# Hybrid decoder layer on one core: projection tiles in halves, larger margins in the written order, second weights asked for earlier

## The chip, the cores and the metric

The kernel runs on one core of a Trainium2 chip. A core has TensorE (PE) for matmuls, VectorE (DVE), ScalarE (ACT) and GpSimd (POOL) for elementwise work, SyncE (SP) for issuing transfers, and 16 DMA engines. Each engine runs its own instruction list in order and waits on semaphores. The metric is device microseconds of one execution. The profile is one execution recorded by the hardware profiler.

## The reference

One layer of a decoder, float32, for a prompt of 512 positions (4 tiles of 128 rows) and for 8 decode requests of one token each, with a past of 4096 positions.

```
h = RMSNorm(x); z = h @ w_in          # 1024 -> 3584 = u_A, v_A, gate_A, q, k, v, gate_B
a = gelu(u_A) * (tril(W_s) @ RMSNorm_group(gelu(v_A)) + b_s)
b = block attention over q, k, v (8 heads x 64, blocks of 256, ALiBi)
y = concat(RMSNorm(a)*silu(gate_A), RMSNorm(b)*silu(gate_B)) @ w_out
out = x + RMSNorm(y)
```

For the prompt the attention is plain causal attention, since there are only two blocks. For a decode request, every head scores the 16 past blocks of 256 positions by q times the mean of K, takes the best three, and attends to these and to the new token. K and V lie in a paged cache and are reached through a page table. So each request needs all its K (8.4 MB) and only the chosen V rows.

## The kernel before, in words

**Prompt.** The seven 512-wide column chunks of `w_in` are worked in the order k, q, v, u, va, ga, gb (steps `pj`, c = 0 to 6), then the two halves of `w_out` (steps `op`). Each is 4 tiles of 128 rows; a tile sums 8 contraction slices into one of two PSUM banks (PA0, PA1). The constant `QUARTERS`, 4, cuts a tile into four pieces of two slices (`pj0` three times, then `pj`, line 980; `op0`, `op`, line 1070). Between pieces TensorE can do other steps. The weights alternate between two buffers, and each chunk comes in four transfers (`WP`) of 512 KB.

**Other TensorE steps.** `kt`, `qk`, `ptr`, `pv` are the prompt's attention (lines 1008, 1026, 1035, 1047); `sg` is the gating matmul (1015); `spj` and `sfd` project the decode tokens and fold the result (934, 994); `spj` needs the chunk's weights.

**Decode requests.** For each request b, GpSimd issues 16 indirect loads, one for each K block (`ld`, line 842), five in flight. VectorE adds the two halves of each block (`ks`, line 704), and TensorE sums four blocks at a time with a window matmul (`gs`, line 1086, four for each request). VectorE forms the gate scores and picks three blocks (`ga`, from line 1469), then `pg` and four `ex` steps multiply the chosen K by q (line 1516), and `sr` reduces (line 1531). The K buffer is then free and `ld` of the next request may start. Softmax follows with `bc` (line 1093), `mt` (1098, VectorE 1550 and 1553) and `mb` (1102), each a small matmul answered by VectorE, and the value matmuls `pv0` and `pv1` (1115). After request 7 come `fin0` to `fin2` and the decode output projection `fop`, `ffd`.

**The order.** `make_plan` writes the order of every engine before the kernel is built. It keeps a clock for each engine and lists of steps (lanes) with assumed durations and dependencies, and always takes the step that could start first; ties go by lane rank. On TensorE the ranks are gate, score, first, attention, side, sample, project. A step of the lanes gate and score is taken only when its data would have been ready for `MARGIN`, 0.3 us; the first three `gs` of a request wait `EARLY_SUMS`, 1.5 us.

```
reach = {"gate": MARGIN, "score": MARGIN, "spread": MARGIN}
...
hold = reach.get(x[1], 0.0) if eng == "PE" else 0.0
if s[0] == "gs" and s[2] < G - 1:
    hold = EARLY_SUMS
start = max(clock[eng], ready + hold)
```

`LANDED` holds assumed arrival times of the first inputs; ("w", 1, 3) is the last piece of the second weights (chunk q), ("w0", x) the pieces of the first. The first are issued by SP right behind the first x tile, in `QUARTERS` transfers, each with its own semaphore. The second are issued by SP in four pieces, each behind the landing of a K block of request 0: blocks 0, 3, 6, 9. Behind these SP has the stores of the k rows and then the spreading of q. Request 0's gate needs the decode tokens' q, made from the second weights by `spj-1` and `sfd-1`, stored and spread over the partitions (`qst`, `qb-0`).

In the order before, TensorE begins so: transposes of x 0 and of the decode rows, two pieces of tile (0,0), transposes of x 1 to 3, `spj-0`, a piece, `sfd-0`, the last piece, a piece of tile (0,1), `gs-0-0`, `kt-0`, two pieces, `gs-0-1`, the last piece, a piece of tile (0,2), `kt-1`, a piece, `gs-0-2`, `spj-1`.

Of the kernel before, what the change touches and what calls it, by code (L numbers as in the profile page):

```python
# [48 lines left out]
def make_plan():  # L49
# [268 lines left out]
    ends, plan = {}, {eng: [] for eng, _ in lanes}  # L318
    for early, at in LANDED:
        ends["Q", early] = at  # L320
# [3 lines left out]
    while True:  # L324
# [35 lines left out]
        if eng == "PE" and bank(s):  # L360
# [10 lines left out]

FLIGHT, WP, EARLY_SUMS, ROOT_HOLD, LANDS = 5, 4, 1.5, 3.0, 1.5
PLAN_START = {"PE": 3.6, "ACT": 2.8, "DVE": 1.0, "POOL": 6.3, "SP": 18.0, "Q": 12.0}
LANDED = [(("x", 0), 4.3), (("x", 1), 10.5), (("x", 2), 12.5), (("x", 3), 14.5), (("xs",), 5.5), (("w", 1, WP - 1), 36.0),
          (("w0", 0), 5.8), (("w0", 1), 7.2), (("w0", 2), 8.6), (("w0", 3), 10.0)]
TILE_US, KEY_US, LAG, MARGIN, SLACK, QUARTERS = 7.4, 1.65, 0.25, 0.3, 0.05, 4
DVE_LANES = "score gate attention groups norm out scale sample tail"
POOL_LANES = "root tiny load fetch"

# [1 line left out]
def hymba_kernel(nc, x_prompt, x_sample, cache_k, cache_v, page_table, g_pre, w_in, sgu_gain, sgu_w,  # L381
# [34 lines left out]
    with ctx:  # L416
# [6 lines left out]
        def sem(name):  # L423
            return ctx.enter_context(nc.semaphore(name))
# [95 lines left out]
        s_k = [sem(f"k_block_loaded{n}") for n in range(NB)]  # L520
# [90 lines left out]
        def load_w(eng, c, x):  # L611

            kcs = slice(x * KC // WP, (x + 1) * KC // WP)
            eng.dma_start(wbuf[:, c % 2, kcs, :], w_src(c)[:, kcs, :]).then_inc(s_w[c % 2], 16)
# [104 lines left out]
        def _(sp):  # L719
# [15 lines left out]
                             (gain[:, :], sgu_gain.rearrange("l g c -> l (g c)").broadcast_to([P, W]))):  # L735
                sp.dma_start(dst, src, allow_slow_non_contiguous=True).then_inc(s_small, 16)
            for x in range(WP):
                sp.wait_ge(s_k[3 * x], 16)
                load_w(sp, 1, x)
            for s in PLAN["SP"]:  # L740
                kind = s[0]
# [889 lines left out]
```

## Time and profile before

| | |
|---|---|
| median of 3 runs | 479.25 us (479.13 to 482.02) |
| the profiled execution | 475.23 us, its span 473.6 us |
| mean granted TensorE clock | 0.936 |
| busy: TensorE, VectorE, GpSimd, ScalarE | 431.6, 283.0, 244.4, 131.8 us |
| weight load (PEld), beside the matmuls | 191.7 us |
| moved by DMA | 110.96 MB, 234 GB/s over the span |

The span runs from the first to the last instruction; the rest of the execution's time lies around it. The two busiest engines are TensorE with 91% and VectorE with 60%. Each group of matmuls in float32 is recorded as two instructions for a contraction slice, so a whole tile is 16 and a quarter 4. Times in the timelines are microseconds from the start of the span.

### The profile page before, as it was taken

The page shows a single profiled execution, that of the slowest core. Times are in us where ns is not written, and L with a number is a line of the kernel's source. Part 1 is how long each engine was busy: PE and PEld are TensorE (multiplying, and loading weights), DVE is VectorE, ACT ScalarE, POOL GpSimd, SP SyncE. Part 2 cuts the span into 40 slices and gives each one's busy share as a digit, 9 for nine tenths or more (in the row PEclk, how much of TensorE's full clock was granted, in tenths as well). Part 3 has the DMA queues.
Part 4 walks back from the last instruction along what each step waited for, and adds up shares of the span by engine and source line. Part 5 has one row for each costly group of instructions (what it writes and reads, how often), then busy time and mean ns, then how long its engine had stood idle before and what let it go on. Part 6 is the DMA issues. An engine that isn't in the chain of part 4 may idle for free.

```text
span 473.6 us, 7936 instructions
## 1 busy us (share of the span) xinstructions
PE 431.6 (91%) x2264; PEld 191.7 (40%) x2264; DVE 283.0 (60%) x749; ACT 131.8 (28%) x295; POOL 244.4 (52%) x344
## 2 busy tenths in 40 slices
PE   6879998999998999898899998997999979969992
PEld 3323443334333544354244544443444434434430
DVE  1534385458445877786476868685746764681334
ACT  3311210101222256224433538524631101000122
POOL 4877115771676167726582576644571666371021
PEclk9997998999998899998699999996599989988997
DMA  8999169994999389759970899349994699451121
GB/s 259 357 391 339 48 201 339 348 265 137 320 360 331 87 284 342 227 165 319 334 226 13 260 360 354 71 99 381 347 316 128 208 381 376 77 103 33 47 90 47
DMA packets 77083, 110.96 MB, mean 234 GB/s; under 512 B 44952, under 2 KB 45464, under 8 KB 77040
## 3 DMA queue, kind: packets, MB, share of 16 engines
q0 software_dynamic: 22576, 71.45, 43.8%
q1 hardware_dynamic: 42768, 21.14, 17.5%
q10 hardware_dynamic: 11696, 17.87, 11.6%
q8 instruction: 18, 0.29, 0.3%
q14 instruction: 25, 0.20, 0.1%
HBM read 106.11 MB, written 4.29 MB: 233 GB/s over the span
## 4 chain that ended last, share of the span: by engine, by line
PE 30%; DMA 29%; DVE 15%; POOL 10%; issue 9%; DVEq 3%; ACT 1%; POOLq 1%; SPq 1%; ACTq 0%
DMA K<-in_cache_k,kidx 23%; PE PA L980 11%; PE PA L1070 8%; POOL K L842 8%; DVE ksum L1516 5%; PE GB L1086 4%; DMA wbuf<-in_w_in 3%; PE SB L934 2%; DVEq L1514 2%; DMA V<-in_page_table 2%; POOL rstd L856 1%; DMA V<-in_cache_v 1%; DVEq L1515 1%; DVE ksum L1469 1%; PE SB L1026 1%
## 5 line engine op out<-in xcount | busy, mean ns | idle before, releaser
L842 POOL DMA_INDIRECT K<-in_cache_k,kidx x128 | 136.4, 1065 | 143.6 <-DVE ksum L1516 73.5
L980 PE MATMUL PA<-wbuf,hT 128*128 128x512 f32 x384 | 184.9, 623 | 0.0
L704 DVE TENSOR_TENSOR ksum<-K 128x512 f32<-128x512 f32 x128 | 87.5, 690 | 85.7 <-DMA K<-in_cache_k,kidx 69.3
L980 PEld LDWEIGHTS PA<-wbuf,hT 128*128 128x128 f32 x384 | 71.3, 197 | 93.0 <-issue 91.0
L689 POOL DMA_DIRECT2D V<-in_cache_v x128 | 75.8, 592 | 30.6 <-issue 17.1
L1070 PE MATMUL PA<-wbuf,hT 128*128 128x512 f32 x128 | 61.7, 629 | 2.4 <-DVE v L1449 2.4
L1516 DVE TENSOR_TENSOR ksum<-K,qb 128x128 f32<-128x128 f32 x192 | 41.7, 285 | 13.4 <-issue 7.1
L1086 PE MATMUL GB<-ksum,win 128*32 128x512 f32 x256 | 37.6, 662 | 8.0 <-DVE ksum L704 7.8
L1070 PEld LDWEIGHTS PA<-wbuf,hT 128*128 128x128 f32 x128 | 24.3, 200 | 32.9 <-issue 32.4
L980 PE MATMUL PA<-hT,wbuf 128*128 128x512 f32 x64 | 31.1, 630 | 0.0
L1026 PE MATMUL SB<-kT,qT 64*128 64x128 f32 (+3 forms) x64 | 28.7, 534 | 0.8 <-DVE pr L1422 0.8
L1531 DVE TENSOR_REDUCE sc<-ksum 128x48 f32<-128x3072 f32 x8 | 26.8, 3353 | 0.3
L1259 ACT ACTIVATE pr<-pr,smax 128x128 f32<-128x128 f32 (+3 forms) x32 | 17.9, 560 | 30.6 <-DVE smax L1425 30.1
L855 POOL TENSOR_SCALAR rstd<-msum 128x1 f32<-128x1 f32 (+3 forms) x18 | 5.6, 310 | 39.5 <-DVE msum L1452 32.4
L1047 PEld LDWEIGHTS PO<-v,pT 128*128 128x128 f32 x160 | 22.6, 209 | 5.5 <-issue 5.4
L1047 PE MATMUL PO<-v,pT 128*128 128x64 f32 x160 | 23.6, 283 | 0.0
L934 PE MATMUL SB<-wbuf,hTs 128*32 128x512 f32 x144 | 19.0, 649 | 2.4 <-DMA wbuf<-in_w_in 2.4
L1267 ACT COPY pT<-SB 128x128 f32<-128x128 f32 (+3 forms) x32 | 13.4, 422 | 27.4 <-PE SB L1035 27.1
L1259 ACT ACT_TABLE_LOAD x13 | 16.7, 1283 | 7.5 <-PE PA L980 7.2
L980 PEld LDWEIGHTS PA<-hT,wbuf 128*128 128x128 f32 x64 | 11.8, 195 | 15.3 <-issue 15.3
L1035 PE MATMUL SB<-ident,pr 128*128 128x128 f32 x80 | 16.6, 309 | 1.3 <-ACT pr L1259 0.9
L1086 PEld LDWEIGHTS GB<-ksum,win 128*32 128x32 f32 x256 | 5.2, 112 | 30.7 <-DVE ksum L704 18.3
(186 smaller groups left out, 376.8 us busy)
## 6 DMA issues: line engine op xcount, KB each, us to landing
wbuf<-in_w_in ACTq DMA_DIRECT2D x20, 512.0 KB, 6.5
V<-in_cache_v SPq DMA_DIRECT2D x240, 32.0 KB
wbuf<-in_w_in SPq DMA_DIRECT2D x8, 512.0 KB, 8.5
V<-in_cache_v POOLq DMA_DIRECT2D x128, 32.0 KB, 2.6
wbuf<-in_w_out ACTq DMA_DIRECT2D x8, 512.0 KB, 8.8
K<-in_cache_k,kidx POOLq DMA_INDIRECT x128, 8.6
qb<-q_rows SPq DMA_DIRECT2D x8, 256.0 KB, 7.2
ya<-in_x_prompt SPq DMA_DIRECT2D x2, 512.0 KB, 7.0
```

Of the source, the lines that this page charges most:

```text
L689: eng.dma_start(V[j * ROWS:(j + 1) * ROWS, h * TOP + k, :, :], v_pages[bass.ds(page, 1), :, :, h * HD:(h + 1) * HD] .rearrange("a p r d -> ...
L704: eng.tensor_tensor(ksum[:, n % SUMS, :], K[:, n, 0, :], K[:, n, 1, :], ALU.add).then_inc(s_dsum, 1)
L842: pool.indirect_dma_start(K[:, n, :, :].rearrange("p r w -> p (r w)"), None, k_rows, bass.IndirectOffsetOnAxis(ap=kidx[:, b, n:n + 1], axis=0)
L934: last = pe.matmul(bank[32 * j:32 * j + 32, :], src[:, kc, :], w[:, kc, :], start=(kc < 4), stop=(kc >= 4), tile_position=(0, 32 * j))
L980: last = pe.matmul(bank[:, :], lhs, rhs, start=(kc == 0), stop=(kc == KC - 1))
L1026: sb_filled(pe.matmul(bank[:, 0:(i + 1) * P], qT[o:o + HD, h // 2, i * P:(i + 1) * P], kT[o:o + HD, h // 2, 0:(i + 1) * P], start=True, st ...
L1047: last = pe.matmul(PO[:, i * HD:(i + 1) * HD], pT[:, a % 2, jt, :], v[:, jt, h * HD:(h + 1) * HD], start=(jt == 0), stop=(jt == i))
L1070: last = pe.matmul(bank[:, :], hT[:, kc, t * P:(t + 1) * P], wbuf[:, c % 2, kc, :], start=(kc == 0), stop=(kc == KC - 1))
L1086: last = pe.matmul(GB[32 * j:32 * j + 32, :], win[:, 31 - g:63 - g], ksum[:, (4 * g + j) % SUMS, :], start=(g == 0), stop=(g == G - 1), ti ...
L1259: act.activation(pr[:, a % 2, 0:(i + 1) * P], pr[:, a % 2, 0:(i + 1) * P], ACT.Exp, bias=smax[:, a % 2:a % 2 + 1], accum_out=ssum[:, h, i: ...
L1516: last = dve.tensor_tensor(kq[:, h * TOP + k, :, :], K[:, bass.ds(n, 1), :, h * HD:(h + 1) * HD] .rearrange("p a r d -> p (a r) d"), qb[:, ...
L1531: dve.tensor_reduce(sc[:, :, :, :].rearrange("p h k r -> p (h k) r"), kq[:, :, :, :], AX.X, ALU.add).then_inc(s_scr, 1)
```

## The change

Three constants and one wait. `QUARTERS` goes from 4 to 2, so a projection tile is two pieces of four slices, and the first weights come in two transfers of 1 MB. `MARGIN` goes from 0.3 to 1.2. `LANDED` has two arrival times for the first weights and 31.0 in place of 36.0 for the last piece of the second. The four pieces of the second weights wait for blocks 0, 2, 4 and 6. The whole order of every engine is written anew from these values.

```diff
-LANDED = [(("x", 0), 4.3), (("x", 1), 10.5), (("x", 2), 12.5), (("x", 3), 14.5), (("xs",), 5.5), (("w", 1, WP - 1), 36.0),
-          (("w0", 0), 5.8), (("w0", 1), 7.2), (("w0", 2), 8.6), (("w0", 3), 10.0)]
-TILE_US, KEY_US, LAG, MARGIN, SLACK, QUARTERS = 7.4, 1.65, 0.25, 0.3, 0.05, 4
+LANDED = [(("x", 0), 4.3), (("x", 1), 10.5), (("x", 2), 12.5), (("x", 3), 14.5), (("xs",), 5.5), (("w", 1, WP - 1), 31.0),
+          (("w0", 0), 6.5), (("w0", 1), 10.0)]
+TILE_US, KEY_US, LAG, MARGIN, SLACK, QUARTERS = 7.4, 1.65, 0.25, 1.2, 0.05, 2
...
             for x in range(WP):
-                sp.wait_ge(s_k[3 * x], 16)
+                sp.wait_ge(s_k[2 * x], 16)
                 load_w(sp, 1, x)
```

## Rows read from the trace of the kernel before

**Rows 1.** Who waited for whom: engine, line, releaser; us in total, times, longest.

```profile
PE GB L1086 <- DVE ksum L704: 7.8, 5, 3.4
PE DC L1102 <- DVE dgm L1553: 7.4, 4, 2.6
PE SB L952 <- DMA ya<-in_x_prompt: 6.1, 2, 4.6
...
PE SB L1035 <- ACT pr L1259: 0.9, 2, 0.5
...
POOL K L842 <- DVE ksum L1516: 73.5, 7, 19.9
```

**Rows 2.** TensorE by stretch: length, busy (instructions), granted clock, DMA share, GB/s.

```profile
0.00:474.00 474.00, 431.63 (x2264) 0.94 0.73 234
...
79.00:83.00 4.00, 4.00 (x16) 0.63 1.05 381
151.00:157.00 6.00, 6.00 (x16) 0.50 0.78 210
223.00:232.00 9.00, 6.15 (x21) 0.50 1.08 338
324.00:341.00 17.00, 16.50 (x46) 0.51 1.06 360
...
424.00:430.00 6.00, 5.21 (x6) 0.50 0.58 113
...
200.00:204.00 4.00, 4.00 (x62) 1.00 0.22 33
```

**Rows 3.** Timeline of TensorE, four stalls: start, duration, instruction, idle before.

```profile
34.92 1.93 PE L1086 MATMUL GB<-ksum,win 128*32 128x512 f32 x8 [3.45 <-DVE ksum L704]
...
150.91 1.94 PE L1086 MATMUL GB<-ksum,win 128*32 128x512 f32 x8 [1.64 <-DVE ksum L704]
198.19 1.07 PE L1086 MATMUL GB<-ksum,win 128*32 128x512 f32 x8 [1.30 <-DVE ksum L704]
...
323.98 0.35 PE L1102 MATMUL DC<-dgm,one 8*128 8x8 f32 x2 [2.59 <-DVE dgm L1553]
```

**Rows 4.** Timeline of VectorE before the stall at 323.98.

```profile
322.34 0.69 DVE L704 TENSOR_TENSOR ksum<-K 128x512 f32<-128x512 f32 x1 [2.91 <-DMA K<-in_cache_k,kidx]
```

**Rows 5.** Timeline, last sums and gate of request 7.

```profile
404.99 0.68 DVE L704 TENSOR_TENSOR ksum<-K 128x512 f32<-128x512 f32 x1
...
408.33 1.06 PE L1086 MATMUL GB<-ksum,win 128*32 128x512 f32 x8
...
409.46 0.69 DVE L1469 TENSOR_TENSOR ksum<-GB,qb 128x512 f32<-128x512 f32 x1 [3.79 <-PE GB L1086]
```

**Rows 6.** First weights' issues (0 to 1.6, 1.6 to 2.2 us; us to landing), then the timeline.

```profile
wbuf<-in_w_in SPq DMA_DIRECT2D x1, 512.0 KB, 5.7
...
wbuf<-in_w_in SPq DMA_DIRECT2D x2, 512.0 KB, 6.9
...
7.46 5.10 PE L980 MATMUL PA<-wbuf,hT 128*128 128x512 f32 x8
...
13.97 1.09 PE L952 MATMUL SB<-ident,ya 128*128 128x128 f32 x8 [1.41 <-DMA ya<-in_x_prompt]
```

**Rows 7.** Timeline around the second weights: SP's issues, a block sum, the decode matmul.

```profile
20.03 17.15 SPq L614 DMA_DIRECT2D wbuf<-in_w_in  x4
...
32.56 0.69 DVE L704 TENSOR_TENSOR ksum<-K 128x512 f32<-128x512 f32 x1 [1.35 <-DMA K<-in_cache_k,kidx]
...
45.12 0.13 PEld L934 LDWEIGHTS SB<-wbuf,hTs 128*32 128x32 f32 x4 [0.30 <-DMA wbuf<-in_w_in]
```

**Rows 8.** Timeline of the tail: the last reduce, the last transposes of decode rows.

```profile
420.69 3.35 DVE L1531 TENSOR_REDUCE sc<-ksum 128x48 f32<-128x3072 f32 x1
...
453.15 0.41 PE L1129 MATMUL SB<-ident,yas 8*128 8x8 f32 x4 [0.21 <-DVE obs L1584]
```

## The prediction

> **What bounds the kernel now.** I read the table of who waited for whom first, because TensorE is busy for 91% of the span and only its waits can be taken away. Its largest waits are those for block sums (VectorE line 704), 7.8 us in 5 stalls, for the softmax maximum (line 1553), 7.4 us in 4 stalls, and for the first rows of x at the head, 6.1 us [rows 1]. The POOL row of the same group shows the second bound. The next request's K blocks may only be issued when the selected K has been multiplied with q, and GpSimd stood 73.5 us over 7 such waits. So there are two long lines of work. One is TensorE's own load. The other is the request loop: 16 K blocks, their sums, the last window matmul `gs` of the request, the gate `ga` on VectorE, the products `ex`, then the next 16 blocks.
>
> The windows come second, because a stall costs more than its length here. Over the span the granted clock is 0.94. In the stretches at 151, 223, 324 and 424 us it is 0.50 to 0.51 (the 1.2 GHz level) for 6, 9, 17 and 6 us [rows 2], and each comes after TensorE had stood. The stretch at 324 us alone is 16.50 us of busy time at half speed, so 8 us of extra time.
>
> Third, the timeline around single stalls. The last sums of requests 2 and 3 were met 1.64 and 1.30 us too early [rows 3]. The maximum step of request 5 was met 2.59 us too early, and the rows of VectorE say why: its queue has a block sum in front of the maximum, which waited 2.91 us for the next request's K block [rows 3, 4]. All four stalls on line 1553 read like this. In the five requests 1, 4, 5, 6 and 7 it is the other way round. In request 7 the last block sum ends at 405.67, the matmul starts at 408.33, and the gate had waited 3.79 us [rows 5]. Read likewise, the five are late by 0.8, 1.4, 0.4, 2.1 and 2.7 us, together 7.3 us. TensorE is thus early for softmax steps and late for most gate steps.
>
> **The change part by part.** No matmul, evacuation or byte is added or removed. What changes is the order on TensorE (with it on the other engines), the split of the first weight transfer, and when the second weights are asked for.
>
> **A. Head, first weights in two transfers.** The first quarter is issued at 1.37 and lands 5.7 us later, at 7.1. The second row is a median over that one and the next, so the second took about 8.1 us and landed near 10.0 [rows 6]. With halves the first projection waits for both, so it starts near 10.0 in place of 7.46, 2.5 us late. The cover: TensorE next needs x rows that came at 13.97, and it stood 1.41 us for them [rows 6]. The eight half-tile matmuls took 5.10 us, so they end near 15.1, 1.1 us after the x rows. What is left of that is covered by the 3.45 us stall before the matmul at 34.92 [rows 3]. Price 0 here; without that cover, 1.1 us.
>
> The Trainium skill, "Perfetto Trace Analysis", section DMA Optimizations, says that splitting transfers into smaller pieces may let some start sooner, which speaks against this part. By that rule alone the head would lose the 2.5 us; the trace agrees that the quarter came earlier, and shows the two covers above.
>
> **B. Second weights with blocks 0, 2, 4, 6.** SP issued the four pieces between 20.03 and 37.18, the last when block 9 had come, at about 36.8 [rows 7]. Block 6 was summed at 32.56, but with one more 512 KB piece ahead of it it comes some 1.3 us later (my estimate: K blocks came 1.3 to 2 us apart around there, and the queues share the same engines), so the last piece is issued near 33.9. The decode matmul `spj-1` waited for it until 45.12, 8.3 us after its issue [rows 7]. The same latency gives 42.1. Working the planner's rule over the first two tiles, I find `spj-1` directly behind `gs-0-1` and tile (0,1), where before half a tile and `gs-0-2` stood between. TensorE gets there near 37.5 to 38, so it would stand about 4 us for weights. In exchange the stall at `gs-0-1` shrinks from 3.45 to about 1: tile (0,1) is complete before it (1.8 us of cover), A adds about 1, and the block itself is up to 1.3 us later. Sum of A and B: +1.5 us; ends -3 (the order keeps it covered and q is spread sooner) and +5. Krow stores behind the four waits on SP move forward by about 3 us and nobody waits for them there.
>
> **C. Softmax steps 0.9 us further out, thrice in a row.** `bc`, `mt` and `mb` each get 1.2 in place of 0.3, so `mb` is planned up to 2.7 us later against the same VectorE work. The four stalls were 1.7, 0.7, 2.6 and 2.4. I take 5.5 of the 7.4 us [rows 1] away (ends 0 and 7.4). Nothing is queued behind them except the value matmuls of the same request, whose results are only needed at the end.
>
> **D. Last sums of a request.** The two early stalls (2.94 us) shrink to about 1: -2 (ends 0 and -2.9). `EARLY_SUMS`, the hold for the first three sums, is unchanged.
>
> **E. The same matmuls where TensorE is late.** Each may now come 0.9 us later by the margin and on average 0.9 us later by the coarser grid (half of 3.7 less half of 1.85). Over 7 loops that is at most 12.6 us in the request loop, and nothing if all fall well. This delay reaches the end only where TensorE has nothing else. After the last reduce ends at 424.04, 49.5 us follow [rows 8], mostly projections. The dependent chain alone I put at some 35 us: about 7 for the softmax and value steps, 13 for the output rows and their norm up to the transposes at 453.15 [rows 8], and 15 of the 20 us behind these, since in them three quarters of a projection stand between the decode steps. So the loop has about 15 us of room, and I charge +3 (ends 0 and 12.6).
>
> **F. Coarser grid for all small steps.** Attention, decode and evacuation steps can enter only at 3.7 us intervals. VectorE and ScalarE stand longer, at places a two-bank ring runs dry, and the last decode steps interleave with halves. +4.5 us: 1.5 at the tail (one more quarter between `fin2` and the end), 3 in the middle (ends 0 and 10). The trace of before has no half tile, so this is the term I know least; the middle value lies near the low end since attention made TensorE wait 0.9 us in all on line 1035 [rows 1].
>
> **G. Clock.** The slow stretches near the stalls of C and D are those at 151 and 324 us, 6 and 17 us, one of 3 us at 79 (0.63 over 4 us) [rows 2] and one like it at 383. They hold 29 us, of which half, some 15 us, is lost. New stalls will bring slow stretches elsewhere. I take half back: -8 (ends 0 and -15).
>
> Sum: 1.5 - 5.5 - 2 + 3 + 4.5 - 8 = -6.5 us. The profiled execution took 475.23 us, so 468.7 for a like one. It lies 0.8% under the median of the runs shown; against the median of 479.25 the same step gives 472.75, and I write 472.8.
>
> **The rivals.**
>
> *Nothing is left of it.* The stalls of C and D are replaced by equal ones at weights and ring slots, and the clock falls as often. For it: all slow stretches but the one at 223 us begin behind a wait of 1.6 to 3.5 us, and B makes a new one of 4. Against it: the margin acts on four stalls with one clear cause. A sum near 0, 476 to 482.
>
> *The request loop becomes the bound (slower).* Place: the last window matmul of each request, `gs-b-3`, in front of the gate. Price: 12.6 us of E in full, with A and B 1.5, tail 1.5, less C and D 7.5, with no help from the clock: +8.1, 487. It decides if the loop falls behind by more than TensorE's work left can fill, that is if the stretch from the last reduce to the end stays near 49.5 us instead of shrinking. For it: in five of seven loops TensorE was late already [rows 5]. Against it: the 15 us of room.
>
> *The clock stays up.* If the mid-kernel stalls fall under what drops the clock, C and D give 8, G gives 15, and F costs 3: -20, so 459. For it: after the 1.30 us stall at 198.19 [rows 3] the clock stayed at full speed [rows 2]. Against it: after one of 1.64 us at 150.91 it fell.
>
> The Trainium skill, "TensorE: Matmul & The Clock Gate", section HAM oscillation, says that a kernel which keeps waiting for transfers pays the slow clock again after each wait; by it B's new wait would bring one slow stretch of its own. The stretch after 34.92 in this trace, where the eight matmuls of a sum took 1.93 us against 1.07 at 198.19 [rows 3], agrees.
>
> *The change doesn't do what it says.* The margins act only through the order; where real times differ from planned ones by more than 2 us a cycle, as they do, the order could fall as badly as before. This is in the first rival.
>
> **How the numbers follow.** My forecast 0.40, nothing left 0.22, loop-bound 0.25, clock stays up 0.13. About 1% (4.8 us) is what a measurement here can tell. The forecast's own range is 466 to 478. Faster by over 1%: most of the forecast (0.34) and the clock case (0.13), and a little of the rest, 0.48. Within 1%: 0.22. Slower: the loop case and the bad end of F, 0.30. For 8 in 10 the range takes in most of both outer cases: 461 to 488.
>
> **What would show it.** Right: line 1553 waits under 3 us in total on TensorE; no slow stretch of 17 us in the middle; a wait of a few us for the second weights near 40; the stretch after the last reduce shorter than 49.5 by what the loop is later. Wrong: the last reduce ends after 430 with 49 us behind it; or waits for ring slots, weights or attention steps on TensorE of over 8 us; or slow stretches that still sum to 50 us.

## The result: slower by 6.3%, and where the time went

The changed kernel takes 508.56 us (median of 4), the kernel before 479.31: ratio 1.063, interval 1.057 to 1.069. Medians here and below are over all runs of a session, while each ratio compares only runs in the faster of the two states that executions fall into, so the two do not divide out exactly, least of all against the 477.74 us of e5 to e8 (the three faster runs of the kernel before lay there at 469.4 to 473.2). I had forecast 472.8 in a range of 461 to 488. The profiled execution took 506.43 us with a span of 504.8, so 31.2 us of span were lost.

The page of the changed kernel, busy time by engine and then the span in 40 slices of 12.6 us (tenths busy, granted clock):

```profile
PE 437.2 (87%) x2264; PEld 198.4 (39%) x2264; DVE 283.1 (56%) x749; ACT 133.9 (27%) x296; POOL 243.3 (48%) x344
...
PE   5979999996999979979997999999638534999994
...
PEclk9997999998999979989999999979955555899998
```

The instruction counts are the same to one, and VectorE, ScalarE and GpSimd are busy within about 2 us of before. TensorE is busy 5.6 us longer (437.2 against 431.6) and idle 25.6 us longer (67.6 against 42.0), together the 31.2. One place shows it: slices 29 to 34. TensorE by stretch, in the changed kernel (length, busy, granted clock, DMA share, GB/s):

```profile
240.00:300.00 60.00, 56.57 (x328) 1.00 0.88 267
300.00:360.00 60.00, 58.98 (x350) 0.94 0.75 224
360.00:420.00 60.00, 29.01 (x243) 0.53 0.84 254
420.00:480.00 60.00, 56.08 (x268) 0.90 0.07 16
...
365.00:405.00 40.00, 22.28 (x81) 0.50 0.93 291
405.00:430.00 25.00, 11.04 (x127) 0.50 0.54 139
```

and in the kernel before:

```profile
300.00:360.00 60.00, 56.91 (x299) 0.86 0.81 254
360.00:420.00 60.00, 56.47 (x363) 0.97 0.69 214
```

Up to 360 the changed kernel is no worse: TensorE is idle 25.2 us there, before 25.7. Between 360 and 420 TensorE is idle 31.0 us against 3.5, so 27.5 us of the 31.2 are lost in this one stretch, and most of what it does there it does at 1.2 GHz (granted clock 0.53).

Who waited for whom on TensorE, the longest of the changed kernel (total, times, longest), beside [rows 1]:

```profile
PE SB L1035 <- issue: 10.4, 1, 10.4
PE SB L1056 <- DVE yb L1380: 7.7, 1, 7.7
PE GB L1086 <- DVE ksum L704: 7.0, 2, 6.6
PE PA L980 <- issue: 4.7, 6, 1.1
PE SB L952 <- DMA ya<-in_x_prompt: 4.6, 1, 4.6
PE SB L934 <- DMA wbuf<-in_w_in: 4.0, 1, 4.0
...
PE DC L1102 <- issue: 0.2, 1, 0.2
```

The maximum step, line 1102, cost 7.4 us in [rows 1] and costs 0.2 now. Three new waits, 10.4, 6.6 and 7.7 us, stand in the bad stretch (the 6.6 and 7.7 at 405.19 and 422.68). For the first the profile names no releaser ("issue"); the timeline gives it. First stretch, the gate and the products of request 6 on VectorE, then an attention step behind them:

```profile
357.28 0.69 DVE L1469 TENSOR_TENSOR ksum<-GB,qb 128x512 f32<-128x512 f32 x1 [3.62 <-PE GB L1086]
...
368.98 3.35 DVE L1531 TENSOR_REDUCE sc<-ksum 128x48 f32<-128x3072 f32 x1
...
372.25 0.68 DVE L1422 SCALAR_TENSOR_TENSOR pr<-alibi,SB 128x512 f32<-128x512 f32 x1
...
373.69 0.72 ACT L1259 ACTIVATE pr<-pr,smax 128x512 f32<-128x512 f32 x1 [11.94 <-DVE smax L1425]
...
374.55 1.11 PE L1035 MATMUL SB<-ident,pr 128*128 128x128 f32 x4 [10.40 <-issue]
```

From 357.28 to 372.33 VectorE is in `ga`, `ex` and `sr` of request 6. The next attention step needs VectorE and then ScalarE, so attention stands for most of these 15 us. In the kernel before TensorE spends the same stretch on projection tiles, since its attention has ended at 349.70:

```profile
349.70 0.42 DVE L1434 TENSOR_TENSOR yb<-PO,rinv 128x256 f32<-128x256 f32 x1
...
356.78 3.70 PE L980 MATMUL PA<-wbuf,hT 128*128 128x512 f32 x8
...
365.66 7.13 PE L980 MATMUL PA<-wbuf,hT 128*128 128x512 f32 x16
...
384.67 7.66 PE L1070 MATMUL PA<-wbuf,hT 128*128 128x512 f32 x16
```

In the changed kernel all 28 tiles of `w_in` are done at 356.2, and there is nothing to run: 10.40 us idle. Second stretch, the end of attention (line 1434 writes the last head) and what follows it:

```profile
396.74 0.42 DVE L1434 TENSOR_TENSOR yb<-PO,rinv 128x256 f32<-128x256 f32 x1
...
404.38 1.30 POOL L689 DMA_DIRECT2D V<-in_cache_v  x2 [0.48 <-issue]
...
410.06 0.23 POOL L855 TENSOR_SCALAR rstd<-msum 128x4 f32<-128x4 f32 x1
...
418.61 3.35 DVE L1531 TENSOR_REDUCE sc<-ksum 128x48 f32<-128x3072 f32 x1
...
421.88 1.41 DVE L1380 SCALAR_TENSOR_TENSOR yb<-yb,rstd,vn 128x512 f32<-128x512 f32 x2
...
422.68 1.12 PE L1056 MATMUL SB<-ident,ya 128*128 128x128 f32 x4 [7.74 <-DVE yb L1380]
...
428.55 3.75 PE L1070 MATMUL PA<-wbuf,hT 128*128 128x512 f32 x4 [1.24 <-ACT vn L1222]
```

The last head is written at 396.7 (349.7 in the kernel before). Its norm stands on GpSimd behind the V fetches of request 6 until 410, and the gating stands on VectorE behind `ga` to `sr` of request 7 until 421.9. The first output matmul comes at 428.6; before it came at 384.7, as shown above. The last reduce ends at 421.96, 2.1 us earlier than in [rows 8], but 82.8 us follow it in place of 49.5, because all eight output tiles are still to do.

### The profile page after: what moved, and what is told of

Read it like the earlier page. It is cut to its first block, busy times and chain, and to the rows that moved or that the text cites. A ratio compares the mean times of both kernels' runs of the same rounds, so it can differ in the third digit from the quotient of the medians.

```text
span 504.8 us, 7934 instructions
## 1 busy us (share of the span) xinstructions
PE 437.2 (87%) x2264; PEld 198.4 (39%) x2264; DVE 283.1 (56%) x749; ACT 133.9 (27%) x296; POOL 243.3 (48%) x344
## 3 DMA queue, kind: packets, MB, share of 16 engines
q1 hardware_dynamic: 42736, 21.14, 15.6%
## 4 chain that ended last, share of the span: by engine, by line
PE 55%; DMA 18%; issue 9%; DVE 7%; POOL 6%; ACTq 2%; DVEq 1%; POOLq 1%; ACT 0%
PE PA L980 26%; DMA K<-in_cache_k,kidx 13%; PE PA L1070 12%; PE GB L1086 4%; POOL K L842 4%; PE SB L934 4%; DVE ksum L1516 3%; PE SB L1026 2%; ACTq L689 2%; DMA V<-in_cache_v 2%; DMA wbuf<-in_w_in 2%; DMA V<-in_page_table 1%; PE SB L994 1%; PE PO L1047 1%; PE DC L1115 1%
## 5 line engine op out<-in xcount | busy, mean ns | idle before, releaser
L842 POOL DMA_INDIRECT K<-in_cache_k,kidx x128 | 133.5, 1043 | 145.7 <-DVE ksum L1516 83.8
L980 PE MATMUL PA<-wbuf,hT 128*128 128x512 f32 x384 | 181.6, 618 | 5.9 <-issue 4.7
L704 DVE TENSOR_TENSOR ksum<-K 128x512 f32<-128x512 f32 x128 | 86.1, 689 | 81.3 <-DMA K<-in_cache_k,kidx 56.0
L1070 PE MATMUL PA<-wbuf,hT 128*128 128x512 f32 x128 | 59.4, 615 | 1.2 <-ACT vn L1222 1.2
L980 PE MATMUL PA<-hT,wbuf 128*128 128x512 f32 x64 | 29.2, 601 | 0.0
L1047 PE MATMUL PO<-v,pT 128*128 128x64 f32 x160 | 26.0, 303 | 2.1 <-issue 1.3
L1047 PEld LDWEIGHTS PO<-v,pT 128*128 128x128 f32 x160 | 24.3, 224 | 8.2 <-issue 7.1
L934 PE MATMUL SB<-wbuf,hTs 128*32 128x512 f32 x144 | 22.4, 750 | 4.7 <-DMA wbuf<-in_w_in 4.0
L1035 PE MATMUL SB<-ident,pr 128*128 128x128 f32 x80 | 17.3, 319 | 10.4 <-issue 10.4
L1035 PEld LDWEIGHTS SB<-ident,pr 128*128 128x128 f32 x80 | 9.5, 153 | 27.5 <-issue 25.5
L1422 DVE SCALAR_TENSOR_TENSOR pr<-alibi,SB 128x128 f32<-128x128 f32 (+3 forms) x32 | 15.4, 482 | 8.0 <-PE SB L1026 7.6
L1115 PE MATMUL DC<-V,pex 128*32 128x64 f32 x768 | 16.7, 232 | 3.2 <-issue 1.8
```

Source lines behind the costliest of these rows:

```text
L704: eng.tensor_tensor(ksum[:, n % SUMS, :], K[:, n, 0, :], K[:, n, 1, :], ALU.add).then_inc(s_dsum, 1)
L842: pool.indirect_dma_start(K[:, n, :, :].rearrange("p r w -> p (r w)"), None, k_rows, bass.IndirectOffsetOnAxis(ap=kidx[:, b, n:n + 1], axis=0)
L934: last = pe.matmul(bank[32 * j:32 * j + 32, :], src[:, kc, :], w[:, kc, :], start=(kc < 4), stop=(kc >= 4), tile_position=(0, 32 * j))
L980: last = pe.matmul(bank[:, :], lhs, rhs, start=(kc == 0), stop=(kc == KC - 1))
L1035: last = pe.transpose(bank[:, jt * P:(jt + 1) * P], pr[:, a % 2, jt * P:(jt + 1) * P], ident[:, :])
L1047: last = pe.matmul(PO[:, i * HD:(i + 1) * HD], pT[:, a % 2, jt, :], v[:, jt, h * HD:(h + 1) * HD], start=(jt == 0), stop=(jt == i))
```

## The experiments

Each ran beside the kernel before on the same chip. Two theories were set against each other. **A**: the loss comes of attention ending when no projection tile is left; the grid and the margin matter only by the order that they lead to. **B**: the coarse grid as such. C (the margin lengthens the request loop) and D (the weights collide) were the others. In all but e6 the whole order is planned anew, so a run tests a constant together with the order that it leads to. Most intervals are 1.3% to either side; neighbours that lie closer are not told apart.

**One part at a time.**

```diff
# e1: QUARTERS 4 -> 2, LANDED ("w0") two values
# e2: MARGIN 0.3 -> 1.2
# e3: LANDED ("w", 1, 3) 36.0 -> 31.0; sp.wait_ge(s_k[3 * x], 16) -> s_k[2 * x]
# e4: e1 and e2 together
```

> Only the tiles in halves; margin 0.3 and second weights behind blocks 0, 3, 6, 9 as before. Theory A (attention ends late): what cost 6% is that in the changed kernel the last attention step stands behind all 28 tiles of w_in, so nothing is left to run beside it, and the output tiles wait for it. In this order the last attention step has 25.5 tiles before it (24.75 before the change, 28 after it), so it costs little: +0 to +2%, the time from the last reduce to the end 50 to 58 us. Rival B (coarse grid as such: every short step waits up to 3.7 us): most of the loss stands here, +4 to +6%. Rival C (margin): same as before within 1%.

Measured 495.12 us against 479.92: ratio 1.033 (1.019 to 1.048). Between A and B. The last reduce ended at 446.6, 22.6 us later than in [rows 8], with 48.9 us behind it. So here the request loop is longer. Part of the reading is that of [rows 5], worse: the last sums are late in every request but the second, by 22.0 us in total against 7.5 before, measured the same way. In request 7 the last block sum ends at 425.79 and the matmul starts 5.1 us later:

```profile
425.11 0.69 DVE L704 TENSOR_TENSOR ksum<-K 128x512 f32<-128x512 f32 x1 [0.99 <-DMA K<-in_cache_k,kidx]
...
430.88 1.06 PE L1086 MATMUL GB<-ksum,win 128*32 128x512 f32 x8
...
432.01 0.69 DVE L1469 TENSOR_TENSOR ksum<-GB,qb 128x512 f32<-128x512 f32 x1 [2.73 <-PE GB L1086]
```

Two other waits stand in this kernel; the profile names no engine as the releaser of either, and the timeline gives it. At 246.66 VectorE had stood 13.38 us for the maximum matmul `mt` of request 3, with block sums of the next request behind it in its queue; the gates of requests 3 and 4 lie 61.1 us apart, before 52.2. At 337.32 TensorE had stood 8.23 us for an attention step, while VectorE was in the gate and the products of request 5 (320.03 to 335.1), although projection tiles were left further back in its queue:

```profile
246.66 0.28 DVE L1550 TENSOR_REDUCE mrow<-DC 8x1 f32<-8x128 f32 x1 [13.38 <-remote]
...
337.32 1.11 PE L1035 MATMUL SB<-ident,pr 128*128 128x128 f32 x4 [8.23 <-issue]
```

> Only the margin 1.2, tiles in quarters. Theory A: the last attention step has 26.25 tiles before it, bc of the last request 33.25; within 1.5% of before. Rival C (margin delays the last sums of each request, the loop of K loads gets longer by up to 7 us): last reduce at 431 or later and +1.5 to +3%. Rival B: within 1%. All: waits on line 1553 on TensorE under 3 us in place of 7.4.

477.25 against 479.92: 0.997 (0.991 to 1.003). C is out: the last reduce ends at 423.7. The margin does to the waits what I wanted, 2.1 us are left on line 1102 and 2.6 on block sums (7.4 and 7.8 before), but the time does not follow.

> Only the second weights behind blocks 0, 2, 4, 6 and their planned arrival 31. All theories A, B, C: within 1% of before; first gate at 53 to 57 us. Rival D (the earlier weights take bandwidth from K blocks and TensorE stands for them): +1 to +2%, a wait of 2 us or more for the second weights near 40 us.

468.75 against 479.92: 0.978 (0.968 to 0.988). All theories missed this; the second weights asked for earlier, with the order planned from it, are a gain of about 2%. The first gate started at 52.1 in place of 56.7, and from there the loop kept 3 to 5 us of lead in most requests (last reduce 420.7). That lead is less than the 2.2% (some 10 us); where the rest comes from is not shown. Line 1102 cost 12.0 us of waits in this kernel, more than before, and it is one of the two fastest: those waits do not decide the time.

> The whole change but for the second weights. Theory A: the last attention step has 27.5 tiles before it and bc of the last request 32.5 (28 in the changed kernel), so output tiles run before the last request's softmax; +1 to +3%, clearly less than the whole change. Rivals B and C (the loss comes of grid and margin as such): +6%, as the whole change.

497.87 against 479.92: 1.042 (1.030 to 1.055). More than A's range by one point, less than the whole change. Attention ended at 380.5, the last reduce at 436.0.

**Quarters beside attention only.** Against the changed kernel:

```diff
+def pieces(c):
+    return 4 if 3 <= c < 7 else 2
...
-            for x in range(QUARTERS):
-                s = ("pj", c, t) if x == last else ("pj0", c, t, x)
+            for x in range(pieces(c)):
+                s = ("pj", c, t) if x == pieces(c) - 1 else ("pj0", c, t, x)
```

(and the same in the output tiles, the durations and the slices of the matmuls.)

> The changed kernel with the tiles of the four chunks u, va, ga, gb (those beside which attention runs) in quarters again; k, q, v and the output tiles stay in halves. Last attention step behind 26.5 tiles of 28, last request's bc behind 33.5 (28 and 28 in the changed kernel). Theory A (the loss is attention ending behind all tiles of w_in): most of it comes back, 0.98 to 1.015 of before; TensorE busy over 50 us of the 60 from 360 on (29 in the changed kernel); stretch from last reduce to the end about 50 us, not 83. Rival B (halves cost wherever they stand): still +3% or more. Rival C (margin): still +4 to +6%.

484.36 against 477.74: 1.032 (1.018 to 1.046). About half of the loss comes back, so by the number rival B holds (+3% or more). The signs of A appear, its price does not: TensorE is busy 52.98 of the 60 us from 360 on, the last head is written at 362.0, and the stretch after the last reduce (431.1) is 52 us. The rest is the loop, 7 us later than before. So A is one part, and what the halves do to the loop a second.

**The steps behind attention moved by hand.** Against the changed kernel:

```diff
+    move("POOL", [("root", 1)], ("fetch", 6, 0, 2))
+    move("ACT", [("pj", 6, 2), ("pj", 6, 3), ("op", 0, 0)], ("pv0", 6))
+    move("DVE", [("pj", 6, 0), ("pj", 6, 1)] + yts + [("pj", 6, 2), ("pj", 6, 3)], ("ga", 7))
+    move("PE", yts + [("op0", 0, 0, 0), ("op", 0, 0)], ("pv0", 6))
+    move("PE", [("op0", 1, 0, 0), ("op", 1, 0)], ("pv1", 6))
```

> The changed kernel, with only steps near the end moved by hand: the norm of the attention rows on GpSimd (root-1) in front of the V fetches of request 6, the gating of the four yb tiles and two transposes in front of the last gate on VectorE, two output tiles in front of the value matmuls of request 6 on TensorE. Theory A with its second part (after attention ended at 396.7 the output tiles stood 26 us in queues behind V fetches and behind the last gate): first output matmul near 412 in place of 428.5 and 8 to 15 us back, ratio to before 1.03 to 1.045. Rival (the tail is bound by the last request's softmax and output rows): within 1% of the changed kernel, 1.055 or more.

499.26 against 477.74: 1.057 (1.043 to 1.071). The place behaved as expected: first output matmul at 412.2. The time did not follow, and the ratio's interval overlaps that of the changed kernel. The gate of request 7 now started at 414.4, 7.7 us after its last block sum, since the moved gating and the copies behind it stood in front of it on VectorE (407.9 to 414.4; only 1.25 us of it was a wait for the norm). The stretch behind the last reduce shrank from 82.8 to 70.8 us, and 6.7 us of that were paid in the loop (last reduce 428.6). The queues behind attention are thus not a cause that can be taken away by themselves.

**Attention held late in the kernel before.** Quarters, margin 0.3 and old weights; one dependency added to `qk` of step 24 (head 6) or 28 (head 7):

```diff
             add("PE", "attention", s, 0.15 + 0.22 * (i + 1), ("ACT", ("kt", NT - 1)),
+                *([("PE", ("pj", 6, 3))] if a == 24 else []),
```

> The kernel before (quarters, margin 0.3, old weights), with attention heads 6 and 7 held until tile 28 is done. That alone puts root-1 behind the V fetches of request 6 and the gating behind the last gate, as in the changed kernel. Theory A: +4 to +7% although tiles are in quarters, over 25 us of TensorE idle between 360 and 425. Rival B or C: about as before, +0 to +2%.

502.44 against 477.74: 1.065 (1.055 to 1.076), the same as the whole change within the intervals. 27 attention steps stand behind tile 28 here, 19 in the changed kernel. With no half tile in it, this kernel has the same picture:

```profile
360.00:420.00 60.00, 32.18 (x316) 0.63 0.83 258
```

```profile
404.66 0.43 DVE L1434 TENSOR_TENSOR yb<-PO,rinv 128x256 f32<-128x256 f32 x1
...
418.04 0.23 POOL L855 TENSOR_SCALAR rstd<-msum 128x4 f32<-128x4 f32 x1
418.09 3.35 DVE L1531 TENSOR_REDUCE sc<-ksum 128x48 f32<-128x3072 f32 x1
...
421.36 1.41 DVE L1380 SCALAR_TENSOR_TENSOR yb<-yb,rstd,vn 128x512 f32<-128x512 f32 x2
...
428.23 1.19 PE L1070 MATMUL PA<-wbuf,hT 128*128 128x512 f32 x1 [1.58 <-ACT vn L1222]
```

The first view is TensorE's stretch, the second the timeline of the end of attention, to be laid beside the one of the changed kernel: 27.8 us idle, and the first output matmul at 428.2.

> As the last, but only head 7 is held until tile 28 is done; attention also ends behind all 28 tiles, but root-1 stays in front of the V fetches of request 6 and two output tiles stand in front of the last bc. Theory A in its strict form (nothing left to run beside the last attention steps): +1 to +3%. If what counts is the queue of the steps behind attention, +0 to +1.5%. Rivals B, C: as before.

496.81 against 477.74: 1.056 (1.043 to 1.069). More than expected. Holding one head back (15 attention steps behind tile 28) is nearly as dear, although the norm stands in front of the V fetches there. The plain medians of e5 to e8 divide to 1.014, 1.045, 1.052 and 1.040: the order of the four is the same, the sizes are a point or two less certain than the intervals say.

**Weights and margin without halves; eighths; the changed kernel again; quarters in q and v alone.** e9 is e2 and e3 together. e10 is e3 with `QUARTERS` 8 and eight arrival times. e12 is the changed kernel with `pieces(c)` 4 for c = 1 and 2.

> Margin 1.2 and the earlier second weights, tiles in quarters: the change without its halves. Last attention step behind 26.25 tiles, last bc behind 33.25. If the halves are what turns the change into a loss: 0.97 to 1.00 of before (the weights alone gave 0.978, the margin alone 0.997). If margin and weights themselves work against each other: 1.02 or more.

471.80 against 476.02: 0.990 (0.985 to 0.994). The change without its halves is 1% faster than the kernel before; e3 is 2% faster. The two did not run on the same chip, so which of them is best stays open.

> Tiles in eighths, margin 0.3, earlier second weights. The written order puts the last attention step behind 27.4 tiles and the last bc behind 28, though the grid is finer. Theory A (what counts is how many tiles are left when attention ends, not the grid): +1 to +4%. Theory B (coarseness itself is the cost, so finer is better): 0.96 to 0.98 of before.

504.74 against 476.02: 1.061 (1.052 to 1.070). This decides against B as the whole story: the finest grid is as slow as the changed kernel. A expected 1 to 4%, so it is off in size. It is no clean case of A either. Its last head was written at 393.4, but beside tiles: TensorE was busy 30.35 of the 33 us from 360 to 393, at full clock. What it shares with the changed kernel is the second stretch. All eight output tiles stand behind the last gate, 79.1 us follow the last reduce, and once the tiles of `w_in` were done TensorE stood 10.46 us for block sums:

```profile
408.27 1.93 PE L1086 MATMUL GB<-ksum,win 128*32 128x512 f32 x8 [10.46 <-DVE ksum L704]
```

> The changed kernel once more, on the chip of these runs, to set the others beside it: 1.055 to 1.07 of before, over 25 us of TensorE idle between 360 and 420.

508.85 against 476.02, medians; no ratio is given for it. Its four runs spread from 499.5 to 514.0 us, 5 to 8% over that median, so it confirms the loss but not the expected 1.055 to 1.07. TensorE was idle 26.0 us between 360 and 420 in the profiled run, of 513.97 us.

> The changed kernel with only the tiles of q and v in quarters (attention does not run beside them); those beside which attention runs stay in halves, margin and weights as changed. The written order ends attention behind 26.5 tiles and the last bc behind 32.5. Theory A (position of attention's end): well under the changed kernel, +1 to +4%. Theory B (halves beside attention are the cost): within 1.5% of the changed kernel.

492.96 against 476.02: 1.032 (1.020 to 1.045). With halves all through attention, but attention ending at 378.5 with tiles left, about half of the 6.3% is gone. That is A's range; its runs (488.0 to 496.0 us) lie wholly under those of the changed kernel on this chip.

Laid out by the place of two steps in the written order, the last attention step and the last `bc` (tiles of 36 in front of it, 28 being those of `w_in` and 8 the output tiles); times in us from the profiled run of each:

| kernel | pieces | tiles before attention's end | tiles before the last `bc` | last head written | last reduce ends | from there to the end | ratio to before |
|---|---|---|---|---|---|---|---|
| before | 4 | 24.75 | 32 | 349.7 | 424.0 | 49.5 | 1 |
| e3 weights | 4 | 25.5 | 32 | 349.4 | 420.7 | 49.4 | 0.978 |
| e9 weights, margin | 4 | 26.25 | 33.25 | 349.4 | 417.0 | 52.3 | 0.990 |
| e2 margin | 4 | 26.25 | 33.25 | 356.1 | 423.7 | 52.5 | 0.997 |
| e1 halves | 2 | 25.5 | 32 | 392.8 | 446.6 | 48.9 | 1.033 |
| e5 | 2 and 4 | 26.5 | 33.5 | 362.0 | 431.1 | 52.3 | 1.032 |
| e12 | 2 and 4 | 26.5 | 32.5 | 378.5 | 432.9 | 56.7 | 1.032 |
| e4 halves, margin | 2 | 27.5 | 32.5 | 380.5 | 436.0 | 54.9 | 1.042 |
| e8 head 7 held | 4 | 28 | 30 | 390.1 | 429.7 | 63.8 | 1.056 |
| e6 tail moved | 2 | 28 | 30 | 400.2 | 428.6 | 70.8 | 1.057 |
| e10 eighths | 8 | 27.4 | 28 | 393.4 | 425.1 | 79.1 | 1.061 |
| changed | 2 | 28 | 28 | 396.7 | 422.0 | 82.8 | 1.063 |
| e7 heads 6, 7 held | 4 | 28 | 28 | 404.7 | 421.4 | 83.5 | 1.065 |

The table parts the losses by place. Where only 28 to 30 tiles stand before the last `bc`, the kernel loses 6% whatever its pieces, and it loses behind the last reduce: 64 to 84 us follow it in place of 49.5. Where attention ends with tiles left but tiles are halves, all or some (e1, e5, e12, e4), it loses 3 to 4%, mostly in the request loop: the last reduce ends 7 to 23 us later, and 49 to 57 us follow it. Those in quarters with tiles left at attention's end lose nothing.

## Why the prediction was wrong

**The step that failed is F**, the coarser grid for the small steps, and with it the rival that I did not write. I priced it at +3 us in the middle, between 0 and 10, by the short attention waits of [rows 1]. These waits were short because projection tiles lay beside attention. The cost lies in when attention ends: the new order put 19 of the 96 attention steps, the last ones of heads 6 and 7, behind tile 28, and all eight output tiles behind the last `bc`. That took 27.5 us of idle time and a long stretch at the low clock. The upper end of 10 us was no bound. I asked what one step waits for, and not how many tiles are left as cover when the chain of 96 attention steps is over. In [rows 1] and [rows 8] nothing warns of it; the place of the last head and the tiles left behind it (3.25) do, and I gave no row to them. One sign that I had put down for being wrong came true: a wait for an attention step of over 8 us (10.4 on line 1035).

**The gains failed too.** I took 15.5 us off for C, D and G, all of them by the margin. With the margin alone (e2) the waits shrink as planned, and the ratio is 0.997 (0.991 to 1.003). So without F there would have been no gain from that side; the gain that there is came from B, which I had at +1.5.

**A**, the head: the first projection started at 8.89 (I had put 10.0), and it cost nothing, as priced: the next wait for x rows, 1.41 us before, is gone.

**B**: the wait for the second weights came where and as long as worked out, at 38.28 for 4.03 us against "about 4 us near 37.5 to 38":

```profile
38.28 3.64 PE L934 MATMUL SB<-wbuf,hTs 128*32 128x512 f32 x16 [4.03 <-DMA wbuf<-in_w_in]
```

Its sum was wrong in sign. I took +1.5 us, but q is spread sooner too: the first gate starts at 53.5 in place of 56.7, and e3 shows a gain of 2.2%, some 10 us, from this part alone. That is outside the ends that I gave (-3 to +5). I had counted what TensorE waits for at the head, and left out the start of the request loop: in e3 the lead at the first gate is 4.6 us, and 3.4 us of it are still there at the last reduce.

**C** was right about the wait and wrong about its worth: 0.2 of 7.4 us are left on line 1102, but in the changed kernel 6.7 us stand at the steps next to it (3.99 on line 1093 at 121.33, 2.68 on line 1098 at 180.34), and in e2 the time does not follow. **D** failed in size: the stalls for block sums are still 7.0 us, though two and not five; one of them is the 6.57 us stall in the bad stretch. **E** was right for the whole change, where the last reduce ends 2.1 us earlier, but by luck of this order: with halves alone it ends 22.6 us later. The 15 us of room that I gave it did not show either: in e1, e5 and e12 the last reduce ends 22.6, 7.0 and 8.8 us later, and the spans are 21.9, 9.8 and 16.0 us longer than before. The "loop becomes the bound" rival is what e1 shows, at 3.3%, not what the whole change shows.

**G**: I expected the slow stretches to shrink. The one of 17 us at 324 was milder (0.80 in place of 0.51 over the same 17 us), but a new one held from 365 to 430. The rival "the clock stays up" was wrong.

The loss of 31.2 us in the sum's own terms: F 27.5 of idle time in one stretch; the busy time grew by 5.6 us over all, and idle time elsewhere shrank by 1.9.

Settled by the runs: attention ending behind the tiles costs about what the change cost, with quarters too (e7, e8); the margin costs nothing and gains nothing, the weights gain. The two causes do not add up: lateness alone costs 6.5% (e7), halves alone 3.3% (e1), the whole change 6.3%. Not settled: why halves cost 3% where attention does end in time (e1, e5, e12). Most of it is lost in the request loop. The last sums of a request are late there by 22.0, 19.1 and 22.3 us over 8 requests, against 7.5 before; but they are late by 19.3 us in the changed kernel as well, whose last reduce ends 2.1 us earlier than before, so that alone does not make the loop longer. Before the last gate VectorE stood 19.3, 17.6 and 10.0 us for softmax matmuls of TensorE, against 2.8 before, but 16.8 in the changed kernel and 15.6 in e7. No run took one of the two away. Also not tried is an order that keeps some tiles in reserve on purpose.

## What to carry to other kernels

Before an order is made coarser, look for the chain that runs beside the big matmuls and ask how many of them are left when it ends. While some are left, and stand in front of the waiting step in the written order, its waits are covered (0.9 us in all on line 1035 before; but 8.2 us at once in e1, where they stood behind it). Once none is left, each wait of the chain is the machine's, and the steps behind it fall in with whatever else is due. A written order that comes out of a planner like this one jumps: take the parts of a change one by one, since here one of three was a gain (0.978), one cost nothing (0.997), one cost 3% (1.033), and the whole was 1.063.

## What the hardware showed that I had not expected

The granted clock stayed at 0.50 from 365 to 430 us in the changed kernel though TensorE was busy 22.28 of 40 and 11.04 of 25 us. TensorE by stretch (length, busy, granted clock, DMA share, GB/s):

```profile
360.00:364.00 4.00, 1.61 (x56) 1.00 0.64 175
364.00:374.50 10.50, 0.16 (x2) 0.51 0.63 195
...
430.00:435.00 5.00, 5.00 (x11) 0.76 0.00 0
435.00:440.00 5.00, 5.00 (x65) 1.00 0.00 0
```

It fell during the wait of 10.40 us. The work that followed, transposes and attention and decode matmuls, mostly with gaps, did not bring it back, not even from 374.5 to 380, where TensorE was busy 5.45 of 5.5 us at 0.50. It rose once the output tiles ran one behind the other. The Trainium skill, "TensorE: Matmul & The Clock Gate", section HAM oscillation, describes a kernel that idles between groups of matmuls and pays the slow clock again each time; this trace agrees, with the difference that here it does not swing but stays down for 65 us.
